# Turning the first feed-forward's tiles with 32x32 transposes on VectorE and a round trip through DRAM instead of matmuls on TensorE

## The reference, cut to what matters

```python
def conv_ffn(h, w_up, conv_w, conv_b, w_down):        # w_up: 2048 x 11264, w_down: 5632 x 2048
    seq = h.shape[1]
    up = h @ w_up
    padded = jnp.pad(up, ((0, 0), (CONV_WIDTH - 1, 0), (0, 0)))   # CONV_WIDTH = 3
    y = conv_b + conv_w[0] * padded[:, 0:seq]
    for tap in range(1, CONV_WIDTH):
        y = y + conv_w[tap] * padded[:, tap:tap + seq]
    gate, val = jnp.split(y, 2, axis=-1)
    return (jax.nn.silu(gate) * val) @ w_down
...
        h = h + mixed
        h = h + conv_ffn(rms_norm(h, ffn_norm[i]), ffn_w_up[i], ffn_conv_w[i], ffn_conv_b[i], ffn_w_down[i])
```

## Time and profile before

| | before |
|---|---|
| time, median of 3 runs | 2618.57 us |
| the profiled execution | 2617.49 us, its span 2615.4 us |
| TensorE busy | 99% of the span |
| VectorE busy | 60% |
| ScalarE busy | 48% |
| first DMA queue, share of 16 engines | 58.6%, 183 GB/s in all |
| granted TensorE clock | full in nearly every slice |

### The profile page before, as it was taken

The page is one execution under the profiler, slowest core; times in us unless marked ns, Lnnn a source line. Parts: engine busy times, 40 slices in busy tenths (PEclk is TensorE's granted clock), DMA queues, the critical chain, the costliest instruction groups (busy, mean ns, idle before and its releaser), DMA issues.

```text
span 2615.4 us, 33124 instructions
## 1 busy us (share of the span) xinstructions
PE 2586.4 (99%) x11995; PEld 2154.3 (82%) x11995; DVE 1579.4 (60%) x1762; ACT 1247.4 (48%) x1586; POOL 39.1 (1%) x44
## 2 busy tenths in 40 slices
PE   7999999999999999999999999999999999999998
PEld 6888888888888888888888888888888888888886
DVE  4565555666666666675766545456555656565555
ACT  5545555544544445454343645454444444444444
POOL 0000000000000000000000000000000000000000
PEclk9999999999999999999999999999999999999999
DMA  6665555666665556656545665665666666666664
GB/s 199 227 183 170 169 168 176 196 187 189 186 188 188 186 184 191 187 177 178 160 144 171 192 177 161 184 191 186 186 203 187 190 188 189 189 189 190 188 190 138
DMA packets 247987, 478.64 MB, mean 183 GB/s; under 512 B 16779, under 2 KB 17635, under 8 KB 247779
## 3 DMA queue, kind: packets, MB, share of 16 engines
q1 hardware_dynamic: 243200, 469.82, 58.6%
q10 hardware_dynamic: 4019, 4.58, 0.5%
q0 software_dynamic: 688, 3.15, 0.4%
HBM read 475.37 MB, written 2.12 MB: 183 GB/s over the span
## 4 chain that ended last, share of the span: by engine, by line
PE 99%; ACTq 0%; ACT 0%; DVE 0%; issue 0%; POOL 0%; POOLq 0%
PE acc L400 31%; PE acc L402 31%; PE acc L401 31%; PE acc L413 2%; PE acc L630 1%; PE acc L473 1%; PE acc L480 0%; ACTq L853 0%; PE acc L490 0%; PE acc L502 0%; PE acc L503 0%; PE acc L657 0%; PE acc L678 0%; PE acc L674 0%; ACT w_hi L795 0%
## 5 line engine op out<-in xcount | busy, mean ns | idle before, releaser
L1177 DVE TENSOR_TENSOR w_lo<-raw,w_hi 128x1024 fp32r<-128x1024 f32 x888 | 1082.4, 1224 | 860.2 <-ACT w_hi L795 858.5
L795 ACT ACTIVATE w_hi<-raw 128x1024 fp32r<-128x1024 f32 x888 | 935.6, 1059 | 1072.1 <-PE acc L402 1052.1
L400 PE MATMUL acc<-w_hi,A_hi 128*128 128x512 f32 x1952 | 771.9, 395 | 1.1 <-issue 1.1
L402 PE MATMUL acc<-w_hi,A_lo 128*128 128x512 f32 x1952 | 760.9, 390 | 0.0
L401 PE MATMUL acc<-w_lo,A_hi 128*128 128x512 f32 x1952 | 760.6, 390 | 0.0
L402 PEld LDWEIGHTS acc<-w_hi,A_lo 128*128 128x128 f32 x1952 | 366.6, 188 | 77.3
L400 PEld LDWEIGHTS acc<-w_hi,A_hi 128*128 128x128 f32 x1952 | 367.1, 188 | 75.2 <-issue 1.7
L401 PEld LDWEIGHTS acc<-w_lo,A_hi 128*128 128x128 f32 x1952 | 367.2, 188 | 72.8
L400 PE MATMUL acc<-w_hi,B_hi 128*128 128x512 f32 x800 | 314.8, 394 | 0.0
L402 PE MATMUL acc<-w_hi,B_lo 128*128 128x512 f32 x800 | 311.7, 390 | 0.0
L401 PE MATMUL acc<-w_lo,B_hi 128*128 128x512 f32 x800 | 311.5, 389 | 0.0
(11 more groups left out here) (156 smaller groups left out, 1085.8 us busy)
## 6 DMA issues: line engine op xcount, KB each, us to landing
raw<-in_up SPq DMA_DIRECT2D x304, 512.0 KB, 4.5
raw<-in_w SPq DMA_DIRECT2D x272, 512.0 KB, 3.9
raw<-in_down SPq DMA_DIRECT2D x216, 512.0 KB, 4.0
raw<-in_wo SPq DMA_DIRECT2D x64, 512.0 KB, 3.8
raw<-in_wa SPq DMA_DIRECT2D x16, 512.0 KB, 4.7
raw<-in_wb SPq DMA_DIRECT2D x16, 512.0 KB, 4.2
scratch<-cum_rows ACTq DMA_DIRECT2D x4, 768.0 KB, 7.0
resid<-in_x SPq DMA_DIRECT2D x4, 512.0 KB, 8.9
```

The costliest lines, as they stand in the source:

```text
L400: pe.matmul(o, hi[:, kt, ts], wh, start=first and kk == 0, stop=False)
L402: m = pe.matmul(o, lo[:, kt, ts], wh, start=False, stop=last and kk == SLOT_K - 1)
L795: act.activation(w_hi[:, q % RING, :], raw[:, q % RING, :], ACT.Copy).then_inc(w_hi_ready, 1)
L1177: dve.tensor_tensor(w_lo[:, q % RING, :], raw[:, q % RING, :], f32(w_hi[:, q % RING, :]), ALU.subtract).then_inc(w_lo_ready, 1)
```

## The change

- TensorE does none of the 22 turns of the first feed-forward. Where a half's turn stood there is now at most a wait for its PSUM banks. The down-products move from the banks BK[0], BK[1], BK[0], BK[3] to BK[2], BK[3], BK[2], BK[3], which the turns no longer need; the last 8 slots use BK[0], BK[1], BK[0], BK[3].
- ScalarE's evacuation (now L1031) writes into `up_q` in blocks of 32 columns, and VectorE transposes all 32x32 blocks of the 128x1024 tile in one instruction (`turn_blocks`, L1391): at p == 8 for the gate half, at q == 0 of the following down-slots (after the split there) for the value half.
- SyncE stores the result to DRAM (`turn1_out`, L358, 128 rows of 4 KB) and, once it has landed, reads it back in four DMAs of 32 partitions (`turn1_back`, L367, pieces of 1 KB). Both stand in SyncE's list between the weight loads: the store ahead of the load of slot 15 or 23, the returns ahead of that of slot 17 or of slot 1 of the next pass. SyncE issues in order, so a wait there holds the loads behind it.
- ScalarE copies the returned tile to token order (L990, 128x1024), waits for its own copy, and does the four activations of the tap from SBUF (L995). VectorE's taps (L1401) read SBUF too.
- The gate's convolution moves from p == 10 to p == 14. The value's stays at p == 1, but is at p == 5 in pass 1 and at q == 5 instead of q == 2 of the last down-slots of pass 10.
- The tiles take `unit(0)`, `unit(5)`, `unit(6)`, `unit(7)` of the scratch memory.

The core of the diff:

```diff
+        up_q, up_x, up_t, up_f = unit(0), unit(5), unit(6), unit(7)
+        up_rows = nc.dram_tensor("up_rows", (P, 1024), F32, kind="Internal").ap()
...
+        def by_block(u, t):
+            return u.rearrange("p (b j t q) -> p t j b q", b=4, j=JT, t=TT)[:, t]
+        def from_quads(u):
+            return u.rearrange("p (a m q) -> p m a q", a=4, m=JT * TT)
...
+            def turn1_out(n):
+                sp.wait_ge(up1_block, n + 1)
+                if n:
+                    sp.wait_ge(up1_back, 64 * n)
+                sp.dma_start(up_rows, up_x).then_inc(up1_sent, 16)
+            def turn1_back(n):
+                sp.wait_ge(up1_sent, 16 * (n + 1))
+                if n:
+                    sp.wait_ge(up1_flat, n)
+                rows = up_rows.rearrange("(a p) (b e) -> b p a e", a=4, b=4)
+                for b in range(4):
+                    sp.dma_start(up_t[32 * b:32 * (b + 1), :].rearrange("p (a e) -> p a e", a=4),
+                                 rows[b]).then_inc(up1_back, 16)
...
+            ups1(R3, 0, {15: lambda: turn1_out(0)})
+            ups1(R3 + U1, 1, {1: lambda: turn1_back(0), 7: lambda: turn1_out(1), 9: lambda: turn1_back(1),
+                              15: lambda: turn1_out(2)})
+            downs(R3 + U1, 2 * SPC, a["down1"], 0, {1: lambda: turn1_back(2), 7: lambda: turn1_out(3)})
+            for i in range(2, FFN1):
                 R = R3 + U1 + B3 * (i - 1)
-                ups1(R, i)
-                downs(R, 2 * SPC, a["down1"], i - 1)
-            downs(R4 - 2, 0, a["down1"], FFN1 - 1)
+                ups1(R, i, {1: lambda: turn1_back(2 * i - 1), 15: lambda: turn1_out(2 * i)})
+                downs(R, 2 * SPC, a["down1"], i - 1, {1: lambda: turn1_back(2 * i), 7: lambda: turn1_out(2 * i + 1)})
+            downs(R4 - 2, 0, a["down1"], FFN1 - 1, {1: lambda: turn1_back(2 * FFN1 - 1)})
...
-                    elif p == 1:
-                        pe.wait_ge(up1_out, 2 * i)
-                        turn(halves(stage_q), TN_FFN1 + 2 * i - 1)
-                    if p == 10:
-                        pe.wait_ge(up1_out, 2 * i + 1)
-                        turn(halves(stage_q), TN_FFN1 + 2 * i)
+                    elif p % SPC == 0:
+                        pe.wait_ge(up1_out, 2 * i - 1 + p // SPC)
...
-            def conv_tap(i, half, dst, n):
-                act.wait_ge(turned, n + 1)
+            def conv_tap(i, half, dst):
+                n = 2 * i + half
+                act.wait_ge(up1_back, 64 * (n + 1))
+                if not (isinstance(i, int) and n == 0):
+                    act.wait_ge(conv_dve, n)
+                act.activation(up_f.rearrange("p (m a q) -> p m a q", m=JT * TT, a=4), from_quads(up_t),
+                               ACT.Copy).then_inc(up1_flat, 1)
+                act.wait_ge(up1_flat, n + 1)
                 for j in range(JT):
                     col = JT * i + j + half * (D_FF // P)
-                    m = act.activation(dst[:, j * T:(j + 1) * T], turn_ps[:, j * T:(j + 1) * T], ACT.Identity,
+                    m = act.activation(dst[:, j * T:(j + 1) * T], up_f[:, j * T:(j + 1) * T], ACT.Identity,
                                        scale=conv[:, 2, bass.ds(col, 1)], bias=conv[:, 3, bass.ds(col, 1)])
...
-                        evacuate(stage_q, BK[p // SPC], rstd, RING * R + p + 1, up1_out)
+                        c = p // SPC
+                        if not (first and c == 0):
+                            act.wait_ge(up1_block, 2 * i + c)
+                        act.wait_ge(slot_done, RING * R + p + 1)
+                        for t in range(TT):
+                            m = act.activation(by_block(up_q, t), acc[:, BK[c][t], :].rearrange("p (j b q) -> p j b q", j=JT, b=4),
+                                               ACT.Copy, scale=rstd[:, t:t + 1])
+                        m.then_inc(up1_out, 1)
...
-                if q == 2:
+                if q == 5:
                     act.wait_ge(gated, FFN1 - 1)
                     conv_value(FFN1 - 1)
-                if q == 3:
+                if q == 6:
                     gated_value(FFN1 - 1, B_hi)
...
+            def turn_blocks(n, first=False):
+                dve.wait_ge(up1_out, n + 1)
+                if not first:
+                    dve.wait_ge(up1_sent, 16 * n)
+                dve.transpose(up_x, up_q).then_inc(up1_block, 1)
...
+                    if p == 14:
+                        conv_taps(i, 0, g_T)
                         dve.wait_ge(gate_sig, i + 1)
                         chain.link(dve.tensor_tensor(g_T, g_T, s_T, ALU.mult))
+                    if p == SPC:
+                        turn_blocks(2 * i, first)
...
-            downs(R4 - 4, 0, D1_BANKS, down1_out, steps=lambda q: value_steps(q - 2, FFN1 - 1, B_hi, B_lo))
+            downs(R4 - 4, 0, D1_BANKS, down1_out, steps=lambda q: value_steps(q - 5, FFN1 - 1, B_hi, B_lo),
+                  turn=2 * FFN1 - 1)
```

More of the change, by code:

```diff
@@ L979, in ups1 @@
                         act.wait_ge(rstd_ready, 2)
-                    if not first and p == 1:
+                    if not first and p == at:
                         act.wait_ge(slot_done, RING * R)
                         conv_value(i - 1)
-                    if not first and p == 2:
+                    if not first and p == at + 1:
                         gated_value(i - 1)
-                    if p == 10:
+                    if p == 14:
                         if not first:
                             act.wait_ge(product, i)
-                        conv_tap(i, 0, g_T, TN_FFN1 + 2 * i)
-                        act.wait_ge(turn_dve, TN_FFN1 + 2 * i + 1)
+                        conv_tap(i, 0, g_T)
+                        act.wait_ge(conv_dve, 2 * i + 1)
                         act.activation(s_T, g_T, ACT.Sigmoid).then_inc(gate_sig, 1)
                     if p % SPC == SPC - 1:
-                        if not (first and p < SPC):
-                            act.wait_ge(turned, TN_FFN1 + 2 * i + p // SPC)
-                        evacuate(stage_q, BK[p // SPC], rstd, RING * R + p + 1, up1_out)
+                        c = p // SPC
[6 more added lines that the diff above has]
+                        m.then_inc(up1_out, 1)
             ups1(R3, 0, first=True)
-            with act.Fori(1, FFN1 - 1) as i:
+            ups1(R3 + U1, 1, at=5)
+            for q in range(2 * NCH):
+                split(R3 + U1, 2 * SPC + q)
+            with act.Fori(2, FFN1 - 1) as i:
                 R = R3 + U1 + B3 * (i - 1)
@@ L1377, in ups1, with downs @@
                         sum_squares(1)
-                    if not first and 1 <= p <= 3:
-                        value_steps(p - 1, i - 1)
-                    if p == 10:
-                        conv_taps(i, 0, g_T, TN_FFN1 + 2 * i)
+                    if not first and at <= p <= at + 2:
+                        value_steps(p - at, i - 1)
+                    if p == 14:
+                        conv_taps(i, 0, g_T)
                         dve.wait_ge(gate_sig, i + 1)
                         chain.link(dve.tensor_tensor(g_T, g_T, s_T, ALU.mult))
-            def downs(R, p0, banks, done, ahead=True, steps=None):
+                    if p == SPC:
+                        turn_blocks(2 * i, first)
+                if first:
+                    turn_blocks(1)
+            def downs(R, p0, banks, done, ahead=True, steps=None, turn=None):
                 for q in range(2 * NCH):
@@ L1388, in downs @@
                         split(R, p0 + q)
+                    if turn is not None and q == 0:
+                        turn_blocks(turn)
                     if steps:
@@ L1394, in _ @@
             ups1(R3, 0, first=True)
-            with dve.Fori(1, FFN1 - 1) as i:
-                chain.enter(i, 1, 3)
+            ups1(R3 + U1, 1, at=5)
+            downs(R3 + U1, 2 * SPC, D1_BANKS, down1_out, turn=3)
+            with dve.Fori(2, FFN1 - 1) as i:
+                chain.enter(i, 2, 3)
                 R = R3 + U1 + B3 * (i - 1)
                 ups1(R, i)
-                downs(R, 2 * SPC, D1_BANKS, down1_out)
-                chain.leave(FFN1 - 2)
+                downs(R, 2 * SPC, D1_BANKS, down1_out, turn=2 * i + 1)
+                chain.leave(FFN1 - 3)
             ups1(R4 - 2 - B3, FFN1 - 1)
-            downs(R4 - 4, 0, D1_BANKS, down1_out, steps=lambda q: value_steps(q - 2, FFN1 - 1, B_hi, B_lo))
+            downs(R4 - 4, 0, D1_BANKS, down1_out, steps=lambda q: value_steps(q - 5, FFN1 - 1, B_hi, B_lo),
+                  turn=2 * FFN1 - 1)
             def down1_steps(q):
@@ L1407, in down1_steps @@
                     operand(TN_DOWN1 + m, A_hi, A_lo, m * JT, G_MIX2)
-            downs(R4 - 2, 0, D1_BANKS, down1_out, steps=down1_steps)
+            downs(R4 - 2, 0, D1_LAST, down1_out, steps=down1_steps)
             def blocks_of(u, h):
```

54 lines of the change are left out of this document (27 added, 27 removed).

## The result

The changed kernel is slower: 2640.26 us (2635.67 to 2644.45) against 2618.70 us (2618.24 to 2619.14) for the kernel before on the same chip, four runs of each. The ratio is 1.0081, interval 1.0068 to 1.0094. That is 21.6 us more, twice the 10.3 that were predicted; the range 2614 to 2658 holds it. The runs of after also lie 9 us apart where those of before lie within 1 us.

What follows compares the result with a forecast made beforehand. TensorE, busy 2586.4 of 2615.4 us, bounds the kernel. -19.4 + 8.1 + 0 + 10.6 + 5.3 + 3.3 + 2.4 = +10.3 us gives 2627.8, with 1.1 for the median 2628.9 us; range 2614 to 2658.

Steps and rivals of the forecast that it cites:

- the four places: Where the change touches the lists: the gate's place, the value's place, the last value and pass 1.
- the turns: First feed-forward: 22 turns leave TensorE, 0.88 us each, -19.4 us in all.
- pass 1: Once: pass 0's value data and SyncE's loads come late, and the gate waits longer; +5.3 us, from 2 to 7.
- rival 3: VectorE's transpose takes two passes, 2.3 us each, so stores and loads go later: +22, 2651 us; chance 0.08.
- The gate's place: 11 times, in front of slot 18: margin 1.25 less 0.88 and 1.11, so TensorE waits 0.74 each, +8.1 us.
- The value's place: Slot 6, passes 2 to 10: margin 2.43 less 0.88 and 1.11 leaves 0.44; no wait, 0 us.
- the trip's delay: 11 gates: the load for slot 17 has margin zero behind the round trip; 0.3 us each, +3.3 us.
- rival 4: Slow returns: load 17 is 1.7 us later at 11 gates, the value's place waits too; 2656 us, chance 0.20.
- The last value: Last downs of pass 10, from q == 5: longer chain and late data make TensorE wait once, +10.6 us.
- the upper bound: The last value's wait with a landing of 7.0 us: 13 us.
- The clock: After long waits TensorE resumes at half clock: 1.6 us at the last value, half in pass 1; +2.4 us.

Runs made afterwards that it cites:

- experiment 5: Changed kernel with the gate's sigmoid on ScalarE and its product on VectorE one step later (p == 15): 2626.08 us, ratio 1.0029.
- experiment 6: Changed kernel with only the value half of block 10 turned by TensorE again, at q == 2 of the down-slots: 2627.42 us, ratio 1.0030.
- experiment 9: Changed kernel with the edits of experiment 5 and experiment 6, and the value's C_hi and C_lo one step later: 2605.20 us, ratio 0.9949.
- experiment 10: Kernel of experiment 9 with block 0's value half also turned by TensorE, at p == 1 of pass 1: 2603.64 us, ratio 0.9945.
- experiment 7: Kernel before, with one transpose instead of eight in each of the first feed-forward's 22 turns: 2601.89 us, ratio 0.9933.
- experiment 1: Changed kernel without store and returns; ScalarE's copy reads the transposed tile directly, in the wrong order: 2622.93 us, ratio 1.0016.
- experiment 4: Changed kernel; SyncE stores the tile and reads 512 KB of a weight matrix, nobody waits for landings, copy reads the transposed tile: 2635.98 us, ratio 1.0060.
- experiment 2: Changed kernel without ScalarE's copy to token order; activations and taps read the returned tile directly, trip kept: 2619.02 us, ratio 0.9999.
- experiment 3: Changed kernel with the trip's store and returns issued by GpSimd instead of SyncE: 2672.09 us, ratio 1.0197.
- the third set: The set of runs that holds experiment 9 and experiment 10; the kernel before took 2618.56 us in it.

## Why the prediction was right, and where its sizes were off

**Direction and mechanism** were right: of the four places that the prediction went through three have a wait as forecast, the fourth, the value's, has one where none was forecast, and experiments 5, 6, 9 and 10 take the four away one by one. Only the turns and pass 1 came out near their price; the other terms were all too small, which is why the sum is half of what was measured. The price of the turns, 0.88, was 0.905 in the table's reading and 0.89 to 0.92 by experiment 7. The transpose takes 1.24 us, so rival 3 falls, and with it the 2.5 us estimated from the Trainium skill's "VectorE: DVE Perf Modes", The three transpose paths: eight transposes at the price of its bf16 one are not what an fp32 tile costs here. The two groups by line (count: ns min, median, max):

```profile
L990 ACT ACTIVATE scratch<-scratch x22: 1041/1044/1061, 457.2 to 1143.0; 128x1024 f32<-128x1024 f32 x22
...
L1391 DVE STREAM_TRANSPOSE scratch<-scratch x22: 1235/1239/1242, 443.1 to 1128.9; 128x1024 f32<-128x1024 f32 x22
...
L995 ACT ACTIVATE scratch<-scratch,conv x88: 583/587/605, 458.3 to 1145.5; 128x256 f32<-128x256 f32 x88
```

**The gate's place, 8.1 predicted, 11.6 without the trip (experiment 1).** The 0.74 agrees with passes 0, 1 and 10 (0.7 each) and is too small for passes 2 to 9 (1.18 each), which ScalarE and VectorE run as a hardware loop while the other three are written out. In the written-out passes the copy starts 1.08 to 1.10 before the first activation, as the predicted 1.11 had it (here at p == 1 of pass 10):

```profile
1081.18 1.04 ACT L990 ACTIVATE scratch<-scratch 128x1024 f32<-128x1024 f32 x1
1082.26 2.08 ACT L995 ACTIVATE scratch<-scratch,conv 128x256 f32<-128x256 f32 x4
```

In the loop it is 1.28 to 1.30 (1048.68 to 1049.97 above). There ScalarE has register instructions of the activations' line behind the wait for the copy, and it sits idle 16 times, twice in each of the eight passes (count: ns min, median, max; then idle us, times):

```profile
L995 ACTq FUSED_REGOPS  x64: 74/74/93, 539.6 to 1050.3; - x64
L995 ACTq ALU_OP  x16: 35/35/35, 539.7 to 1049.9; - x16
...
  ACT scratch L990: 3.9, 16
```

Before, a split ran ahead of the same activations, and the engine idled 0.03 us in front of them. So the copy costs 0.18 more than predicted in the loop, and that is not the wait for its result, which is 0.03 in the written-out passes. The four activations take 2.08 from SBUF, not the 1.92 that the earlier trace rows had from PSUM, which the prediction set equal on the word of VectorE's rows; ScalarE's differ. 0.18 + 0.16 make 1.08 out of 0.74, and the slow start behind a gap another tenth: 1.18, eight times. In passes 0 and 10 the agreement is partly luck: the copy has no such extra there, and the margin before was 1.66, not the 1.25 read in pass 9, which makes up for the activations and the slow start that the prediction left out.

**The value's place, 0 predicted, 9.8 measured.** This is the step that failed, for two reasons. The margin of 2.43 was read in pass 10, the written-out one, and taken for all nine. The same two rows of the kernel before in pass 9 give 1014.27 - 1012.16 = 2.11, and passes 2 to 8 the same within 0.01:

```profile
1010.93 1.23 DVE L1177 TENSOR_TENSOR w_lo<-raw,w_hi 128x1024 fp32r<-128x1024 f32 x1 [2.07 <-ACT w_hi L795]
...
1014.27 0.39 PE L400 MATMUL acc<-w_hi,A_hi 128*128 128x512 f32 x1
```

2.11 less 0.90 for the turn, 1.29 for the copy and 0.16 for the activations is -0.24: TensorE has to wait there without any trip, and it does, 0.3 in each of these eight passes of experiment 1 (2.7 in sum). In pass 10, where 2.43 - 0.90 - 1.08 - 0.16 leaves 0.29, it does not. The other reason is that the prediction put the trip's delay at the gates only (3.3 at that place; 1.8 measured, gates with the trip less gates without). The delay came at slot 6: 7.1 us of the difference to experiment 1. Where the margin is nothing, every late load counts in full, and the prediction gave that price only to rival 4.

**The last value, 12.2 predicted with its clock, 15.7 measured.** The chain was right (14.4 for 14.2), the data's arrival was not: 7.4 after slot 21 starts instead of 4.6. The store landed in 3.0 us, not 4.0, but the four returns took 7.7 us from the last one's issue, where 4.5 was taken, more even than the upper bound's 7.0. The splits in front of the copy were late too (4.86 us of waiting for a load in the row shown), but ScalarE was done with them 1.91 us before the returned tile was there, so the landing alone set the start. Without the trip the place costs 9.4 against 7.3 + 1.6.

**Pass 1, 6.1 predicted with its clock, 6.5 measured**, in the predicted two places: 2.2 at slots 9 and 10 (1.6 predicted) and 5.0 at slot 18, 0.7 of it the gate's. How much of it is SyncE held behind the late transpose, and how much the bytes of three trips in one pass, stays open; experiment 4 keeps both.

**The clock, 2.4 predicted.** After the gap of 13.5 us the windows of TensorE (busy us and instructions, granted clock, DMA share, GB/s) are:

```profile
1144.00:1157.00 13.00, 0.00 (x0) 0.65 0.31 111
1157.00:1161.00 4.00, 3.58 (x9) 0.50 0.55 139
1161.00:1165.00 4.00, 4.00 (x18) 0.94 0.39 128
```

The granted clock is down at 0.50, the 1.2 GHz level, when the matmuls resume, nine of them take 3.6 us, and then it is back at nearly 2.4 GHz. The last value's 15.7 less its wait of 13.5 is 2.2, where 1.6 was predicted. Pass 1's wait of 3.3 us, ahead of 516.78, does it too: the next six matmuls start 0.43 apart from 517.38 on, some 1.4 us lost where half of 1.6 was predicted, and the granted clock is 0.50 here as well:

```profile
517.00:519.00 2.00, 2.00 (x5) 0.50 0.49 113
```

That the array falls back to the lower clock when it idles is what the Trainium skill states ("TensorE: Matmul & The Clock Gate", Part 1: The HAM clock gate), and the trace agrees.

**The trip's transfers** were under-priced as a whole: the parts laid to it (3.3 at the gates, 3.3 of the last value, 6.1 in pass 1) make 12.7, while experiment 1 gives 17.3. What was missed is that not only the load of slot 17 is late. The 1 MB more per half raised the DMA share between 430 and 1130 us from 0.60 to 0.71, while ScalarE's waits for loads went from 10.7 to 146 us, of which 67 are there without any trip (experiment 1). Such late loads cost next to nothing where there is cover (passes 2 to 10 of experiments 2, 9 and 10) and all of it where there is none. They are also the likely reason for the wider spread of after's runs, which is argued and not shown: experiment 7, with no trip, spreads 0.5 us, and experiment 3, with the trip on another engine, 6.5, but the kernel before spreads 5.1 in the third set.

**Rival 4** gave 2656 for returns at half rate. The returns took 5.0 us in the median and up to 9.3, near what 128 KB pieces of a read of weights took in experiment 4 (6.2), and the place it named, slot 6, is where the time went; but a rate of the returns by themselves was not measured. The rule of the Trainium skill behind it ("SBUF — State Buffer", Door 1: The DMA port swizzle) is neither shown nor refuted by these runs.

## What to carry to other kernels

Taking work off the engine that sets the end also takes away the cover which that work gave to the others: before counting the gain, subtract it from the margin of every slot behind which another engine's list grows. Here 19.9 us of transposes went and 45.4 us of waits came, all at four places in the lists; moving two small steps behind the next split and leaving the first and the last half on TensorE, where no time is left to hide a round trip, turned +21.6 us into -14.9. And a margin of about zero is no "no cost": price it with every delay that can reach it, and read it in every kind of pass. Here the written-out pass had 0.3 to 0.4 us more than the looped ones, and waited for nothing at slot 6 where the eight others waited 0.3 each.

## What the runs showed of the hardware beyond what was expected

- An activation that waits for the result of the one before it on ScalarE started 0.03 us after its end in the written-out passes (6 tiles), and 0.24 to 0.26 after it where register instructions of the loop stood between (16 tiles).
- A 128x256 activation took 587 ns with its input in SBUF against 564 ns from PSUM before (medians of 88 each). VectorE's taps took 478 ns against 474 (medians of 176 each).
- The round trip over GpSimd's queue landed later than over SyncE's: the 512 KB store in 5.1 us against 3.0, the four 128 KB returns in 5.7 against 5.0, and the kernel was 32 us slower.
- After a wait of 3.3 us in pass 1 the granted clock was 0.50, and the next six matmuls started 0.43 us apart instead of 0.23.
- An fp32 transpose of all 32x32 blocks of a 128x1024 tile took VectorE 1.24 us, the same as a plain operation of that size.
